# A 512-token forward pass of four layers: parts of the attentions' vector work given to GpSimd, and the first compressed scores issued ahead

## What is computed

```python
for layer in range(2):                       # first_block
    x = x + rmsnorm(mixer(rmsnorm(x)))       # layer 0: "fox" attention and short convolution; layer 1: RG-LRU
    x = x + rmsnorm(memory_cross_attention(rmsnorm(x), rmsnorm(mem)))     # 4 heads of 256, 256 memory rows
    x = x + rmsnorm(swiglu(rmsnorm(x)))
for l in range(2):                           # second_block
    x = layer_norm(ALPHA * x + 0.5 * swiglu_2(x))
    x = layer_norm(ALPHA * x + hybrid_mixer(x))
    x = layer_norm(ALPHA * x + 0.5 * swiglu_2(x))

# in hybrid_mixer, nsa_mixer: 8 heads of 96, 2 groups of keys, per query block
p_cmp = masked_softmax(q @ kc, cmp_end <= t)          # 31 compressed keys
o_cmp = p_cmp @ vc
o_slc = masked_softmax(q @ k_selected) @ v_selected   # with 512 tokens every block is selected
o_win = masked_softmax(q @ k_window) @ v_window       # and the window holds all earlier tokens
o = g[..., 0:1] * o_cmp + g[..., 1:2] * o_slc + g[..., 2:3] * o_win
```

## Time and profile before

| what | value |
|---|---|
| median of 3 runs (lowest, highest) | 3549.33 us (3547.49, 3549.85) |
| the profiled execution, its own time | 3549.51 us |
| its span in the profile | 3547.7 us |
| PE busy | 3485.3 us, 98% |
| DVE busy | 1462.1 us, 41% |
| ACT busy | 1187.2 us, 33% |
| POOL busy | 61.1 us, 2% |

### The profile page before, as it was taken

One profiled execution on the slowest core, in us unless ns is written; L12 is line 12 of the kernel. 1 busy time (PEld: TensorE's weight loads), 2 busy tenths in 40 slices (PEclk: granted clock), 3 DMA queues, 4 the chain that ended last, 5 costly groups with the idle time before them and its releaser, 6 DMA issues.

```text
span 3547.7 us, 39728 instructions
## 1 busy us (share of the span) xinstructions
PE 3485.3 (98%) x17605; PEld 2929.2 (83%) x17605; DVE 1462.1 (41%) x1562; ACT 1187.2 (33%) x1749; POOL 61.1 (2%) x68
## 2 busy tenths in 40 slices
PE   8999999999999999999999999999999999999999
PEld 7888888888788888888888778888888888788887
DVE  4454532347645223333335554323422345552333
ACT  3343422236634222322224343222322233432222
POOL 2000000000000000000000000000000000000000
PEclk9999999999999999999999999999999999999999
DMA  5224232223341322232223103222333223013221
GB/s 158 88 64 150 65 114 95 95 77 101 107 143 66 107 95 95 84 119 95 96 89 110 38 25 107 95 95 102 100 96 102 100 69 96 25 63 104 95 96 59
DMA packets 246333, 326.44 MB, mean 92 GB/s; under 512 B 18320, under 2 KB 215232, under 8 KB 246160
## 3 DMA queue, kind: packets, MB, share of 16 engines
q1 hardware_dynamic: 241232, 308.77, 26.4%
q0 software_dynamic: 4928, 15.12, 1.3%
HBM read 321.74 MB, written 2.10 MB: 91 GB/s over the span
## 4 chain that ended last, share of the span: by engine, by line
PE 91%; DVE 4%; ACT 4%; issue 0%; DMA 0%; SPq 0%; DVEq 0%; ACTq 0%
PE P L506 28%; PE P L508 28%; PE P L507 28%; PE P L511 3%; PE P L641 2%; PE P L666 2%; DVE WR L1483 1%; ACT WR L999 1%; DVE STAT L1596 1%; ACT BIG L1012 1%; ACT BC L1012 1%; DVE BIG L1496 1%; PE P L928 0%; PE P L911 0%; DVE BIG L1505 0%; ACT L1012 0%
## 5 line engine op out<-in xcount | busy, mean ns | idle before, releaser
L1483 DVE TENSOR_TENSOR WR<-STG,WR 128x2048 fp32r<-128x2048 f32 (+3 forms) x324 | 672.8, 2079 | 1359.5 <-ACT WR L999 1359.2
L506 PE MATMUL P<-HT,WR 128*128 128x512 f32 (+1 forms) x3016 | 1123.3, 372 | 4.7 <-DVE WR L1483 3.0
L507 PE MATMUL P<-HT,WR 128*128 128x512 f32 (+1 forms) x3016 | 1120.1, 371 | 0.0
L508 PE MATMUL P<-HT,WR 128*128 128x512 f32 (+1 forms) x3016 | 1120.1, 371 | 0.0
L999 ACT CAST WR<-STG 128x2048 fp32r<-128x2048 f32 (+3 forms) x324 | 561.7, 1735 | 1073.0 <-PE P L508 1072.8
L506 PEld LDWEIGHTS P<-HT,WR 128*128 128x128 f32 x3016 | 569.3, 189 | 103.1 <-DVE WR L1483 4.3
L508 PEld LDWEIGHTS P<-HT,WR 128*128 128x128 f32 x3016 | 569.3, 189 | 98.0
L507 PEld LDWEIGHTS P<-HT,WR 128*128 128x128 f32 x3016 | 569.4, 189 | 96.9
L506 PE MATMUL P<-WR,HT 128*128 128x512 f32 (+1 forms) x1344 | 524.8, 390 | 8.3 <-ACT WR L999 6.6
L508 PE MATMUL P<-WR,HT 128*128 128x512 f32 (+1 forms) x1344 | 521.5, 388 | 0.0
L507 PE MATMUL P<-WR,HT 128*128 128x512 f32 (+1 forms) x1344 | 521.1, 388 | 0.0
(11 more groups left out here) (178 smaller groups left out, 2360.6 us busy)
## 6 DMA issues: line engine op xcount, KB each, us to landing
STG<-in_w_ffn_gu_dram SPq DMA_DIRECT2D x44, 1024.0 KB, 4.9
STG<-in_ffn_w_gate_dram SPq DMA_DIRECT2D x44, 1024.0 KB, 5.1
STG<-in_ffn_w_up_dram SPq DMA_DIRECT2D x44, 1024.0 KB, 5.1
STG<-in_ffn_w_down_dram SPq DMA_DIRECT2D x44, 1024.0 KB, 4.9
STG<-in_w_ffn_down_dram SPq DMA_DIRECT2D x22, 1024.0 KB, 4.8
STG<-in_w_xkv_dram SPq DMA_DIRECT2D x16, 1024.0 KB, 5.3
STG<-in_w_in_dram SPq DMA_DIRECT2D x12, 1024.0 KB, 5.2
STG<-in_w_xq_dram SPq DMA_DIRECT2D x8, 1024.0 KB, 5.1
```

The costliest lines, as they stand in the source:

```text
L506: pe.matmul(o, lh, rh, start=first, stop=False)
L507: pe.matmul(o, lh, rl, start=False, stop=False)
L508: return pe.matmul(o, ll, rh, start=False, stop=last)
L1483: v.tensor_tensor(WR[0:p, n % NWR, 1, cut], STG[0:p, n % NSTG, cut], WR[0:p, n % NWR, 0, cut].bitcast(F32), ALU.subtract).then_inc(ve.sem, ...
```

## The change

Nothing is computed otherwise; nothing is taken out. Five things differ.

1. A new counter `pl` (`pool_done`). The rests of eight weight units, the last parts of `SPLITS`, are made by POOL, each as one instruction over the whole unit, after ACT's fourth part. DVE's `split_part` is gone; ACT's four parts stay at their steps. SP and `take` wait for `pl` on these units.
2. In `finish` of `n`, POOL adds `N_TMP` to `N_ON`. DVE's next write of `N_TMP` waits for that add, and so does PE's turn of the finished block.
3. In the compressed softmax POOL subtracts the maxima and multiplies with the mask, the latter right behind the exponential; DVE's sums, inverse and gate become `weights`, at later steps, on columns 8 to 15 of `STAT` (the maxima keep 0 to 7).
4. The compressed scores of the first block (t = 3) are issued before `attend`, on PE and on DVE, not in step 2; their exponential is in step 1.
5. POOL's DMA issues stand behind the rests in its own order.

```diff
+        by_pool = {U[name] + 3 for name in [("fox", "qk", 2), ("fox", "qk", 3), ("x0", "q", 3), ("x1", "q", 3), ("n0", "v", 0),
+                                            ("n0", "v", 4), ("n1", "v", 0), ("n1", "v", 4)]}
+        low = lambda n: (pl if n in by_pool else ve).at("lo", n)
...
-            parts = {"scores": (2, 9, 23, 37), "norm": (3, 10, 24, 38), "turn": (5, 16, 32, 40), "out": (7, 20, 36, 44)}
+            parts = {"scores": (None, 9, 23, 37), "exp": (1, 9, 23, 37), "turn": (5, 16, 32, 40), "weights": (6, 19, 35, 43),
+                     "out": (7, 20, 36, 44)}
...
+            def lo(name):
+                n = U[name] + 3
+                _, _, p, k, w = units[n]
+                g.wait_ge(*ac.at("hi", n))
+                cut = slice(0, k * w)
+                po.tensor_tensor(WR[0:p, n % NWR, 1, cut], STG[0:p, n % NSTG, cut], WR[0:p, n % NWR, 0, cut].bitcast(F32),
+                                 ALU.subtract).then_inc(pl.sem, pl.up("lo", n))
...
+                def shifted(t):
+                    g.wait_ge(*ve.at(s, "m8", t))
+                    po.tensor_tensor(N_S8, N_S8, M8.unsqueeze(2).broadcast_to([128, 8, 31]),
+                                     ALU.subtract).then_inc(pl.sem, pl.up(s, "s8m", t))
...
+                def weighted(t):
+                    g.wait_ge(*ac.at(s, "e8", t))
+                    po.tensor_tensor(N_S8, N_S8, CMUL[:, t, :].unsqueeze(1).broadcast_to([128, 8, 31]),
+                                     ALU.mult).then_inc(pl.sem, pl.up(s, "p8", t))
...
+                def finished(it, j):
+                    t, br = it["t"], it["br"]
+                    g.wait_ge(*ve.at(s, "on", j))
+                    g.wait_ge(*ve.at(s, "co", t))
+                    po.tensor_tensor(N_ON[:, t % 2, :], N_ON[:, t % 2, :], N_TMP, ALU.add).then_inc(
+                        pl.sem, pl.up(s, "on", t, br))
...
+                for i, it, b_, c_, ends in att_steps(s):
+                    if i == 0:
+                        shifted(ORDER["n"][0])
+                    if c_ and c_["last"]:
+                        finished(c_, i - 3)
+                    if i in SPLITS["n"] and SPLITS["n"][i][1] == 3:
+                        lo((s, *SPLITS["n"][i][0]))
...
-                    g.wait_ge(*ve.at(s, "on", "x", t))
+                    g.wait_ge(*(pl.at(s, "on", t, 1) if s[0] == "n" else ve.at(s, "on", "x", t)))
...
+                scores(ORDER["n"][0])
                 g.wait_ge(*pw_zero.at("zeros", s))
                 last_turn = attend(s, lambda h: ve.at(s, "k", 2), ve.at(s, "v", 3), hook)
...
+                    if br:
+                        g.wait_ge(*pl.at(s, "on", t, 0))
+                    elif earlier(s, t) is not None:
+                        g.wait_ge(*pl.at(s, "on", earlier(s, t), 1))
                     tt(ov4(N_TMP), ov(N_OB(br)), wv(w8), ALU.mult, s, "on", j)
-                    g.wait_ge(*ve.now())
-                    tt(N_ON[:, t % 2, :], N_ON[:, t % 2, :], N_TMP, ALU.add, *((s, "on", "x", t) if br else ()))
```

More of the change, by code:

```diff
@@ L304, in build @@
         N_GT = [BC[0:62, 0, 96 * z:96 * z + 96] for z in range(2)]
+        M8 = STAT[:, 0:8]
         N_GH, N_KCMP = FX[0:96, 0:62], FX[0:96, 64:126]
@@ L427, in gain, with nsa @@
                 po.dma_start(BC[:, i:i + 1, :], src).then_inc(bc[i].sem, bc[i].up(s))
+            def lo(name):
[5 more added lines that the diff above has]
+                                 ALU.subtract).then_inc(pl.sem, pl.up("lo", n))
+            def nsa(l):
+                s = f"n{l}"
+                def shifted(t):
[19 more added lines that the diff above has]
+                        lo((s, *SPLITS["n"][i][0]))
+                    for part, t in nsa_hook(i):
+                        if part == "scores":
+                            shifted(t)
+                        if part == "exp":
+                            weighted(t)
             def memory(l):
@@ L461, in gpsimd @@
                 else:
+                    lo(("fox", "qk", 2))
+                    lo(("fox", "qk", 3))
                     g.wait_ge(*mm.at("fox", "t", len(fox_items()) - 1))
@@ L464, in gpsimd @@
                 gain(1, a, T["g_cross_pre"][l])
+                lo((f"x{l}", "q", 3))
                 g.wait_ge(*mm.at(f"x{l}", "t", 15))
@@ L482, in gpsimd @@
                         po.memset(RB[96:128, 0:3968].bitcast(F32), 0.0).then_inc(pw_zero.sem, pw_zero.up("block_zeros", s))
+                    if part == 1:
+                        nsa(l)
                     g.wait_ge(*(mm.at(s, "t", len(nsa_items()) - 1) if part == 1 else ve.at(before, "x", 3)))
@@ L1455, in tail @@
                     for part, t in nsa_hook(i):
-                        if part == "scores":
+                        if part == "exp":
                             scores(t)
@@ L1477, in vector, with lo, after @@
             g = Gate(v)
-            def lo(n, part=0, of=1):
+            def lo(n):
                 _, _, p, k, w = units[n]
-                g.wait_ge(*ac.at("hi", n, *((part,) if part < of - 1 else ())))
-                cut = slice(part * k * w // of, (part + 1) * k * w // of)
+                g.wait_ge(*ac.at("hi", n))
+                cut = slice(0, k * w)
                 v.tensor_tensor(WR[0:p, n % NWR, 1, cut], STG[0:p, n % NSTG, cut], WR[0:p, n % NWR, 0, cut].bitcast(F32),
-                                ALU.subtract).then_inc(ve.sem, ve.up("lo", n, *((part,) if part < of - 1 else ())))
-            def after(name, part=0, of=1):
+                                ALU.subtract).then_inc(ve.sem, ve.up("lo", n))
+            def after(name):
                 if U[name] + 3 < len(units):
-                    lo(U[name] + 3, part, of)
-            def split_part(s, i):
-                if i in SPLITS[s[0]]:
-                    name, part = SPLITS[s[0]][i]
-                    after((s, *name), part, 4)
+                    lo(U[name] + 3)
             def tt(o, x, y, op, *point):
@@ L2069, in tail @@
                             scores(t)
-                        if part == "norm":
-                            cmp_norm(t)
+                        if part == "weights":
+                            weights(t)
+                scores(ORDER["n"][0])
                 attend(s, finish, hook, tail)
```

37 lines of the change are left out of this document (16 added, 21 removed).

## The result

The changed kernel takes **3517.3 us** (median of four runs, 3516.1 to 3518.4), the kernel before took 3549.6 us (3547.5 to 3551.4) beside it. The ratio is 0.9908, with a 95% interval of 0.9897 to 0.992: 32.3 us faster, where 24.3 were forecast. The profiled execution of the changed kernel took 3518.3 us with 3516.5 of span, 31.2 us less span than before.

A forecast was written before the change was run, and what follows sets the result against it. PE, busy 98% of the span, bounds the kernel, so only idle time and low clock can be won. Gains of n0 9.2, n1 9.1, fox 2.3, clock 5.1, less 1.4, make 24.3 us: 3549.5 to 3525 us, range 3517 to 3538.

The forecast's parts named there:

- Waits for copies: PE's waits for DVE copies in n0 and n1: 3.3 and 2.8 us before products, 3.4 and 3.8 before turns, all gained.
- The bank of step 9: PE's wait for the bank that the mask addition frees: 0.45 of 1.84 us remain, 1.4 gained in n0 and n1 each.
- The entry: Start of each NSA attention, with compressed scores done while PE would wait: 1.1 us gained each, about 1.0 us idle left.
- Fox: Four waits of PE for copies in fox, 3.1 us: three quarters, 2.3 us, gained.
- The clock: Three stretches at lower clock in n0 and n1 lost 6.8 us: two go, one of 1.7 us stays, 5.1 gained.
- The charge of 1.4 us: Cost set against the gains for `weights` beside other DVE bursts and for small waits replacing removed ones: 1.4 us in all.
- POOL's price: POOL's two-operand instructions: 0.43 us for 248 elements, 1.3 for 768, 3.6 for 2048; no cost at the attention's end.
- Signs: What would show it: PE idle 4 to 5 us per NSA attention, no wait above 1.1, DVE 44 less busy, POOL 55 more.
- half of the waits returning: New waits replace removed ones: half of 20.6 us returns, the clock falls as often as before, 3539 us; 20%.
- The exclusive port: DVE instructions reading two SBUF operands, the gate products, stand until POOL's current one is done: 8 us, 3533 us; 10%.
- The full standstill: DVE stands still, whatever it does, while POOL reads SBUF, in steps 12 and 30, fox's 11 and 15: 3557 us; 5%.
- The clock is the larger part: No stretch at 1.2 GHz left and the 1.4 us charge not needed: 3 us more, 3522 us, within the forecast's range.

The follow-up runs named there:

- e1: The kernel before with only the rests of the eight split weight units moved to POOL: 3532.2 us, ratio 0.9952.
- e3: The kernel before with only the compressed softmax's shift and mask on POOL and DVE's sums at later steps: 3542.5 us, ratio 0.9981.
- e6: The changed kernel with the rests made in parts on DVE again: 3531.2 us, ratio 0.9946 to the kernel before.
- e2: The kernel before with only the sixteen branch additions on POOL: 3551.1 us, ratio 1.0004.
- e7: The changed kernel with shift and mask on DVE again, at their earlier steps: 3525.5 us, ratio 0.9932 to the kernel before.
- e9: The changed kernel plus two tiny DVE instructions beside a POOL rest in step 13: a reciprocal, then a product (n0) or copy (n1): 3517.6 us, one run.
- e4: The kernel before with only the first block's compressed scores issued ahead of the attention: 3547.4 us, ratio 0.999.
- e5: The changed kernel with the first compressed scores back in step 2: 3524.9 us, ratio 0.9929 to the kernel before.
- e8: The changed kernel with the branch additions on DVE again: 3519.3 us, ratio 0.9913 to the kernel before.
- e10: The changed kernel with POOL multiplying the same 128x768 tile by ones before each branch addition: 3523.2 us, ratio 0.9923 to the kernel before.

## Why the prediction came out as it did

Sign and mechanism were right, the size was too small: 24.3 us forecast, 31.2 in the profiled execution and 32.3 in the medians. **The step that failed** is the step from a wait to its worth: the sum priced each wait of PE at its idle row, put the rest of its cost at nothing and gave no reason for that. The runs show some 0.2 us more for each, 3.7 us for those that went. Two terms were mis-sized besides: the clock, 5.1 us where 6.8 came, and the charge of 1.4 us, of which nothing came. The low end of the range, 3517, was put at "every wait and all of the clock" with small waits that the sum left standing. Those still stand, so that the time came out there has another reason than the one given. Step by step:

- **Waits for copies**, 3.3 and 2.8 us before products, 3.4 and 3.8 before turns: right, all are gone. e1, e3 and e6 show that they had two causes that add, rests and softmax with finish.
- **The bank of step 9**: right, 0.45 us forecast to remain, 0.39 measured; the like waits of steps 23 and 37 stayed, as said.
- **The entry**: too low. 1.1 us forecast, of which 0.3 for item 3. Measured are 1.84 - 0.67 = 1.17 and the 0.25 of item 3's wait, 1.4 in each of the two.
- **Fox**: 2.3 forecast, 2.7 measured. I let one wait stand as ahead of the first part that is handed over; one did stand, but it was the shortest.
- **The clock**: mis-sized. "I expect two of the three stretches to go and one of 1.7 us to stay, since the entry keeps an idle of 1.0": 6.8 came, not 5.1. The idle left there is 0.67 us in the trace, and in no run with 1.13 us or less at the entry did the clock fall there. That no step was lost elsewhere may be partly luck, since one step can be chance.
- **The charge of 1.4 us** for small waits: failed. No wait came in their place, apart from POOL's 0.23 us at the end; the other small ones were there before. The 0.8 us of idle time that the rest of the program has more are not of this kind.
- **The price of a wait**: the step that was missing. I took a wait for its idle row. It costs 0.23 us more, 3.7 us for the 16 that went. Together with the clock, the charge, fox and the two entries, 1.7 + 1.4 + 3.7 + 0.4 + 0.6 = 7.8 us, less 0.5 for POOL at the two ends and 0.8 of idle time elsewhere, which is 6.5 of the 31.2 - 24.3 = 6.9 us that were missing.
- **POOL's price**: too low, and of no consequence but at the end. The term for it was 0, 0.23 us per attention came. (For 1.7 us per addition the prediction's own reckoning, in which 2.0 cost 0.5, gives 0.2, not the 0.3 written there.)
- **Signs**: DVE is 39 us less busy (44 forecast), POOL 75.5 more busy (55 forecast, from the low price). PE's idle time per attention is 3.6 us (4 to 5 forecast), and no wait is above 1.1.
- **The rivals**: half of the waits returning did not occur (7 waits are left of 13 in each attention, none longer than before). The exclusive port exists (e2, e7, e9) but the change itself keeps clear of it, since it also moves the mask; I had bound it to the gate products, and there it costs less than 0.1 us; the clamps, which I had not thought of, stand for 0.6 us in n0 and cause no wait. The full standstill is refuted by maxima and copies of 0.68 to 0.69 us inside a rest. "The clock is the larger part" is what happened, and its 3522 was 4 to 5 us too high, about the price of the waits.

That the clock shares in what a part is worth is read from one profile each for the pair e4 and e5, not shown beyond that; which idle pattern lets the clock fall stays open. So does whether the end of the attention could be rid of POOL's 0.23 us by leaving only the last addition on DVE.

## What to carry to other kernels

When PE is nearly always busy, look for piles in the queue of the engine that feeds it and not at its average load: here 16.6 us of DVE's work per attention were given to a slower engine at nearly double their price, and PE gained because they left the places where a copy was due. Nearly half of it, the 7.7 us of additions, brought at most 2 us in all. Count a wait of PE at its idle row plus 0.2 us or so, and judge edits on the clock in company: no single edit ended the loss, three together (e8) did. Before work goes to POOL, list the DVE instructions that read two SBUF operands, or copy or scale from SBUF to SBUF, in the steps where POOL reads, since those stand until POOL is done, and move them too.

## What the runs showed of the hardware that I had not expected

- **The clock's loss moves with the pattern of waits.** After an entry wait of 1.84 us it fell in all ten entries that had one (before, e1, e2, e3 and e5, two each), and in none of the eighteen with 1.13 us or less. The eighteen also have the compressed scores in another place, so that the length of the wait is what matters is likely, not shown. But e4, with the shorter entry, lost 8.6 us further on, and e2, with waits of 2.0 us, 10.2.
- **A small DVE instruction can take 3.3 us** beside a POOL instruction of 4.5 us, and shows as a long instruction. Not only products of two operands do so, a copy (e9) and a clamp with a constant (e7, 1.22 instead of 0.17 us) do too, while a reciprocal and a reduction don't. SBUF — State Buffer of the Trainium skill, in the same section, counts copies and scalings among those that can take the shared pair, and the rows agree.
- **POOL's operations have a small fixed part**: 0.60 to 0.67 us for 248 elements, 1.82 for 768 and 4.52 for 2048. Between the last two that is (4.52 - 1.82) / 1280 = 2.1 ns per element, which leaves some 0.1 to 0.2 us at each of the three lengths. With one operand held constant over the row, 768 elements take 1.47 us (e10).
